# A two-layer RWKV-7 and attention step on one core: GpSimd instead of VectorE makes two products of the recurrence's preparation

## What is computed

```python
def step(S, inp):
    r_t, w_t, k_t, v_t, a_t, b_t = inp
    sa = jnp.einsum('bhvk,bhk->bhv', S, a_t)
    S = S * w_t[:, :, None, :] + sa[..., None] * b_t[:, :, None, :] + v_t[..., None] * k_t[:, :, None, :]
    return S, jnp.einsum('bhvk,bhk->bhv', S, r_t)
```

## Time and profile before

| | |
|---|---|
| time, median of 3 runs | 5512.53 us (5505.92 to 5513.2) |
| time of the profiled execution | 5517.87 us |
| its span | 5516.1 us |
| PE busy in the span | 4655.1 us (84%) |
| DVE busy | 1996.5 us (36%) |
| ACT busy | 1822.5 us (33%) |
| POOL busy | 409.9 us (7%) |
| the two recurrences | about 854 to 1556 us and 3595 to 4300 us |
| instructions L456 and L458 | 32 each, 0.686 and 0.685 us |

### The profile page before, as it was taken

One profiled execution on the slowest core, in us unless ns is written; L12 is line 12 of the kernel. 1 busy time (PEld: TensorE's weight loads), 2 busy tenths in 40 slices (PEclk: granted clock), 3 DMA queues, 4 the chain that ended last, 5 costly groups with the idle time before them and its releaser, 6 DMA issues. The chain is left out here.

```text
span 5516.1 us, 118531 instructions
## 1 busy us (share of the span) xinstructions
PE 4655.1 (84%) x49316; PEld 3793.3 (69%) x49316; DVE 1996.5 (36%) x4592; ACT 1822.5 (33%) x3588; POOL 409.9 (7%) x216
## 2 busy tenths in 40 slices
PE   5999996888968887678969999969889688866789
PEld 4999995887845555453459999958888455553533
DVE  3000004555456665331130000055554566643311
ACT  3000004555544553131130000055555444432211
POOL 1222220000000000000022222100000000000000
PEclk9999997999989997689969999979999899976899
DMA  4111111111011101683431111111110111017834
GB/s 159 69 69 69 69 56 54 37 36 39 20 51 39 38 31 56 211 290 111 135 111 69 69 69 69 50 56 31 41 34 19 49 39 38 31 56 227 275 115 133
DMA packets 240533, 444.16 MB, mean 81 GB/s; under 512 B 36594, under 2 KB 133748, under 8 KB 225908
## 3 DMA queue, kind: packets, MB, share of 16 engines
q1 hardware_dynamic: 216900, 323.26, 18.5%
q10 hardware_dynamic: 23232, 115.16, 5.5%
HBM read 314.54 MB, written 132.32 MB: 81 GB/s over the span
## 5 line engine op out<-in xcount | busy, mean ns | idle before, releaser
L1874 PE MATMUL psum<-h_parts,w_parts 128*128 128x416 f32 x2640 | 930.1, 352 | 24.9 <-POOL w_parts L1793 24.9
L1875 PE MATMUL psum<-h_parts,w_parts 128*128 128x416 f32 x2640 | 926.6, 351 | 0.0
L1876 PE MATMUL psum<-h_parts,w_parts 128*128 128x416 f32 x2640 | 925.8, 351 | 0.0
L1836 DVE COPY arena<-psum 128x416 f32<-128x416 f32 x132 | 78.2, 592 | 1433.8 <-PE psum L1876 1433.8
L1758 ACT ACTIVATE arena<-psum 128x416 f32<-128x416 f32 x198 | 102.7, 519 | 1422.2 <-PE psum L1876 1422.2
L1039 PE MATMUL psum<-arena 128*128 128x512 f32 (+3 forms) x1280 | 546.6, 570 | 19.6 <-DVE arena L986 8.1
L1874 PEld LDWEIGHTS psum<-h_parts,w_parts 128*128 128x128 f32 x2640 | 496.3, 188 | 29.6 <-issue 25.2
L1169 PE MATMUL psum<-arena 128*128 128x512 f32 (+1 forms) x1088 | 475.2, 597 | 38.2 <-DMA arena<-x_cur 38.2
L1876 PEld LDWEIGHTS psum<-h_parts,w_parts 128*128 128x128 f32 x2640 | 496.6, 188 | 6.5
L1875 PEld LDWEIGHTS psum<-h_parts,w_parts 128*128 128x128 f32 x2640 | 497.5, 188 | 4.3
L1169 PEld LDWEIGHTS psum<-arena 128*128 128x128 f32 (+1 forms) x1088 | 201.6, 187 | 310.4 <-issue 310.4
(11 more groups left out here) (336 smaller groups left out, 6618.9 us busy)
## 6 DMA issues: line engine op xcount, KB each, us to landing
out_proj_t<-arena ACTq DMA_DIRECT2D x66, 1040.5 KB, 4.1
arena<-in_cache_k SPq DMA_DIRECT2D x256, 256.0 KB, 3.9
arena<-in_cache_v SPq DMA_DIRECT2D x256, 256.0 KB, 4.1
arena<-in_w_in SPq DMA_DIRECT2D x66, 512.0 KB, 3.5
arena<-x_cur SPq DMA_DIRECT2D x64, 512.0 KB, 5.7
arena<-out_proj_t SPq DMA_DIRECT2D x96, 257.0 KB, 3.2
arena<-out_proj_t SPq DMA_DIRECT2D x24, 1024.0 KB, 8.8
arena<-mixed_t SPq DMA_DIRECT2D x32, 512.0 KB, 5.1
```

The source lines that it names most:

```text
L1874: pe.matmul(bank[g][:, 0:TG], w_hi[u][:, k, :], h_hi[:, k, col], start=(k == 0), stop=False)
L1875: pe.matmul(bank[g][:, 0:TG], w_hi[u][:, k, :], h_lo[:, k, col], start=False, stop=False)
L1876: mm = pe.matmul(bank[g][:, 0:TG], w_lo[u][:, k, :], h_hi[:, k, col], start=False, stop=(k == KT - 1))
```

## The change

VectorE's steps `sV_R` and `sV_K` are gone, and GpSimd runs the same two products in a loop over all 16 units. A new semaphore pair `pG` (steps `sG_R`, `sG_K`) stands for them. GpSimd waits for E and for kf ahead of R, for Ei ahead of K, and from unit 6 on for the output of unit `m - 5`, which read the buffer of RA that is written. Everyone who used VectorE's order to know that R and K were made now waits for `pG`.

```diff
@@ rwkv_scalar, rates @@
                 if m:
                     pV.wait(act, m - 1, sV_B)
+                    pG.wait(act, m - 1, sG_K)
@@ rwkv_gpsimd @@
             pool.memset(E[:, :, :, 0:1], 1.0).then_inc(r_once, 1)
+            for m in range(NU):
+                tq, two = m // 2, slice(m % 2 * 2, m % 2 * 2 + 2)
+                pA.wait(pool, m, sA_E)
+                pV.wait(pool, m, sV_KF)
+                if m >= 6:
+                    yAll.wait(pool, m - 5, 1)
+                pG.inc(pool.tensor_tensor(q4(RA[:, tq % 3, two, 0, :]), q4(xr), E[:, :, :, 1:CH + 1], ALU.mult))
+                pA.wait(pool, m, sA_EI)
+                pG.inc(pool.tensor_tensor(Kf[:, tq % 2, two, :], kf[:, :, :], Ei[:, :, :], ALU.mult))
+                pG.close()
@@ rwkv_vector @@
                 pA.wait(dve, m, {sV_XK: sA_CK, sV_XR: sA_CR, sV_XV: sA_CV}[k])
+                if m and k == sV_XR:
+                    pG.wait(dve, m - 1, sG_R)
...
                     pA.wait(dve, m, sA_MM)
+                    if m:
+                        pG.wait(dve, m - 1, sG_K)
                     i_ = dve.tensor_tensor(kf[:, :, :], tw[:, :, :], xk[:, :, :], ALU.mult)
...
-                elif k == sV_R:
-                    i_ = dve.tensor_tensor(q4(RA[:, tq % 3, two, 0, :]), q4(xr), E[:, :, :, 1:CH + 1], ALU.mult)
-                elif k == sV_K:
-                    i_ = dve.tensor_tensor(Kf[:, tq % 2, two, :], kf[:, :, :], Ei[:, :, :], ALU.mult)
...
                 if m is not None:
-                    prep(m, sV_R)
-                    prep(m, sV_K)
                     prep(m, sV_MX)
                     prep(m, sV_RC)
@@ rwkv_tensor @@
                     pV.wait(pe, n // 2 * 2 + 1, sV_B)
+                    pG.wait(pe, n // 2 * 2 + 1, sG_K)
```

More of the change, by code:

```diff
@@ L223, in build @@
         sA_CK, sA_CR, sA_CV, sA_TW, sA_TA, sA_KS, sA_E, sA_EI, sA_MM, sA_SQ = range(1, 11)
-        sV_XK, sV_XR, sV_XV, sV_LD, sV_SCAN, sV_KF, sV_RKB, sV_R, sV_K, sV_MX, sV_RC, sV_KKN, sV_A, sV_BB, sV_B, sV_BV = range(1, 17)
+        sV_XK, sV_XR, sV_XV, sV_LD, sV_SCAN, sV_KF, sV_RKB, sV_MX, sV_RC, sV_KKN, sV_A, sV_BB, sV_B, sV_BV = range(1, 15)
+        sG_R, sG_K = range(1, 3)
         sT_ZW, sT_ZA, sT_SS, sT_RN, sT_BO = range(1, 6)
-        pA, pV, pT = mark("prep_scalar", 10), mark("prep_vector", 16), mark("prep_tensor", 5)
+        pA, pV, pT, pG = mark("prep_scalar", 10), mark("prep_vector", 14), mark("prep_tensor", 5), mark("prep_gpsimd", 2)
         lA, lV = mark("lora_scalar", 2), mark("lora_vector", 1)
```

## The result

The changed kernel takes 5544.97 us (median of 5 runs, 5539.46 to 5548.31) against 5512.53 us (5505.92 to 5514.15) for the kernel before: a ratio of 1.0059, 95% interval 1.0044 to 1.0074, so 24 to 41 us slower. Its profiled execution has a span of 5543.2 us, 27.1 us more than before.

The account below looks back on a forecast made before the run. It took TensorE as setting the pace, waiting on VectorE's L450, L454, L491, L673 chain. 34.8 us of delay, less 1.8, plus 0.5 at the start gave 33.5 us, so 5546 us, range 5505 to 5561.

Parts of the forecast that it names:

- What bounds the kernel, and that R and K return nothing in the steady part: TensorE sets the pace; in steady slots nobody waits for VectorE's R and K, 1.21 us a unit.
- The second L454 waits for R: In 26 slots VectorE's second L454 stands behind GpSimd's R, 1.34 us late, delaying L491 and TensorE; chance 0.46.
- GpSimd's durations: R and K, each 128 x 512 with two full inputs, take 1.26 us each on GpSimd.
- 26 x 1.34 - 1.8 = 33 us for the steady part: Steady-part loss: 26 slots each 1.34 us late, less 1.84 us that VectorE now waits ahead of L491.
- At the start of the pipeline the two amounts cancel, +0.5 us: In four starting units, 1.21 us saved on VectorE against 1.34 us of delay leaves +0.5 us.
- The waits for GpSimd cost nothing: New waits of TensorE, ScalarE and VectorE for GpSimd are fulfilled long before reached, with over 10 us of slack.
- nothing is shared: Rival: GpSimd and VectorE do not interfere, only the pipeline start counts: -5.3 us, 5507 us; chance 0.24.
- By turns within an instruction: Rival: L454 pair and GpSimd both run slower; at worst its 0.88 us doubles, 21 us, 5533; chance 0.14.
- GpSimd keeps its turn: Rival: R and K run back to back, or R precedes the first L454; L491 2.6 us late, 5578; chance 0.09.
- Faster through the clock: Rival: TensorE's clock rises one unit earlier at the pipeline start, with no contention: 5501 us; chance 0.07.

Follow-up runs that it names:

- rc_release: The changed kernel with GpSimd's R and K released by sV_RC (the reciprocal) instead of sV_KF: 5504.46 us against 5512.59, ratio 0.9983.
- k_late: The changed kernel with only GpSimd's K waiting for sV_RC, R still released by sV_KF: 5527.8 us, ratio 1.0031 to the kernel before.
- products_twice: The kernel before, VectorE still making R and K, with GpSimd making both once more into an unread spare tile: 5555.57 us, ratio 1.0082.
- memset_beside: The kernel before with two GpSimd memsets of 704 columns in a spare tile, where the change has R and K: 5510.84 us, ratio 0.9996.
- memset_long: The kernel before with two GpSimd memsets of 1600 columns in a spare tile, released by sV_KF: 5519.32 us against 5514.31, ratio 1.0013.
- mask_first_after: The changed kernel with VectorE's masked(u, 3) put ahead of sV_RKB: 5515.08 us, ratio 1.0013 to the kernel before.
- rkb_release: The changed kernel with GpSimd's R released by sV_RKB instead of sV_KF: 5501.93 us, ratio 0.9989 to the kernel before.

## Why the prediction was right, and where it was not

The time was right, 5546 predicted and 5545 measured, and so were the sign and the mechanism of the steady part. Two of its terms were wrong by about as much in opposite directions, so that the hit to the microsecond is luck.

- **What bounds the kernel, and that R and K return nothing in the steady part:** right. In rc_release, where nothing meets, the gain is 8 us (3 to 15 by the interval), where the prediction has 5.3 us for that case.
- **The second L454 waits for R:** right, in 31 of 32 units. Its size was not. I had it 1.34 us late, because I added R's whole length to the end of the first L454. In 30 of 32 units R starts 0.13 to 0.16 us after the end of sV_KF and so 0.09 to 0.12 us behind the first of the pair, runs beside it, and the second ends 1.80 us after the pair began: 0.92 us late. TensorE's wait for the mask, forecast near 1.6 us, is 1.23.
- **GpSimd's durations:** R and K take 1.18 and 1.27 us where they meet nothing, 1.42 and 1.45 in the change; predicted was 1.26 for both.
- **26 x 1.34 - 1.8 = 33 us for the steady part:** too large. With 0.92 us it is 22 us, and k_late against rc_release shows 23.7 in their traces. Against the kernel before, the stretch from sV_KF of unit 3 to that of unit 15 grew from 483.1 to 489.8 us in layer 1 and from 484.3 to 495.8 in layer 2, by 18.2 us together.
- **At the start of the pipeline the two amounts cancel, +0.5 us:** this is the step that failed. It missed that K meets the clamp. The sum there moved L461 forward by 1.21 us without asking what GpSimd is at by then; K runs until 3.0 us after the end of sV_KF, and VectorE reaches the clamp at 1.8. The prediction's own times have the same overlap: its second L454 would end at 1.74 + 0.48 = 2.22 us, with K at work until 3.0. It had also read from the earlier trace rows that one input can use both ways into SBUF, but looked only for instructions with two inputs. From sV_KF of unit 0 to that of unit 3, layer 1 went from 940.17 - 874.16 = 66.0 us to 945.72 - 873.41 = 72.3, both layers from 131.9 to 143.4. The clamp's own excess is 2 x (3 x 1.06 + 0.46 + 0.14) = 7.6 us.
- **The waits for GpSimd cost nothing:** right. TensorE never waits for L430 or L432 in the trace after.
- **The rivals:** "nothing is shared" is refuted by products_twice against memset_beside. "By turns within an instruction" is refuted by the rows of the pair (L470): the first keeps 0.49 us with R beside it, the second waits. "GpSimd keeps its turn" did not happen; in the slot shown, the pair's second ends at 1190.13, when K has run for 0.31 of its 1.45 us. "Faster through the clock" did not happen.

What the start of the pipeline lost beyond the clamp's own 7.6 us shows in TensorE's clock. From sV_KF of unit 2 to that of unit 3 the change takes 32.6 us in layer 1 and k_late 28.8, and 1.06 of the 3.8 us are the clamp. The same matmuls in the change and then in k_late, with the granted clock of 914 to 920 us ahead of them:

```profile
914.00:920.00 6.00, 4.90 (x44) 4.17 (x46) 3.85 (x7) 2.56 (x5) 2.74 (x2) 0.50 0.00 0
918.97 1.97 PE L867 MATMUL psum<-arena 64*64 64x64 f32 x32
920.73 1.69 PE L873 MATMUL psum<-ident,arena 64*64 64x64 f32 x32
931.92 1.71 PE L683 MATMUL psum<-arena 64*64 64x64 f32 x32 [1.47 <-DVE arena L503]
...
914.00:920.00 6.00, 5.91 (x116) 4.98 (x112) 3.60 (x7) 3.52 (x9) 0.95 (x1) 0.84 0.01 3
915.49 1.34 PE L868 MATMUL psum<-arena 64*64 64x64 f32 x32
916.67 1.10 PE L874 MATMUL psum<-ident,arena 64*64 64x64 f32 x32
927.26 1.15 PE L684 MATMUL psum<-arena 64*64 64x64 f32 x32 [1.47 <-DVE arena L504]
```

In the change TensorE stays at the lower of its two levels (0.50, 1.2 of 2.4 GHz) through L867 and most of L873, 1.2 us more than in k_late, and is there once more from 932 us on, which by the end of that dip makes another 1.5 us. k_late has such a dip too, only after its unit 3 has begun (L684, 1.53 us at 942.68), so the second amount is moved rather than lost; this fits the 3.2 us that come back in the steady part. The granted clock from 914 to 920 us is 0.50 in all three of the change, memset_long and mask_first_after, in which the clamp is held up, and 0.89, 0.84 and 0.72 in the kernel before, k_late and memset_beside, in which it is not. That the clamp's delay is what keeps the clock down is concluded from this pattern, not tested by itself. The traces thus account for some 10 us of K's meeting; what the medians show beyond that (17) is within their error.

The Trainium skill's rule (SBUF — State Buffer, § Who interferes with whom) is borne out in what it says of instructions with two SBUF inputs, held up by GpSimd's products and not by its memsets. It also says that a `tensor_scalar` can take a mode that uses both of VectorE's ports and then contends with GpSimd; the clamp, held up beside products and memsets alike, fits that, but no row shows in which mode it ran. Where the section says that the one that comes second is fully blocked, the traces agree for VectorE. For GpSimd's R, which starts 0.10 us into a first L470 of 0.48 us and was 0.24 us longer (1.42 against 1.18 us), they can't tell: GpSimd's rows do not show when it first reaches for SBUF.

## What to carry to other kernels

Moving work to an idle GpSimd does not make it free: ask which VectorE instructions will run beside it, and what waits for those. Here those with two SBUF inputs and the clamp, a `tensor_scalar` between SBUF tiles, were held up for the rest of GpSimd's instruction, while the reciprocal between SBUF tiles and those that read PSUM and one SBUF tile went on. The same two products cost 32 us or gained 8 by the placing of one wait, so choose GpSimd's release for the gap that VectorE's own list of instructions shows, and check the first and last units of a pipeline apart from the steady ones.

## What the runs showed of the hardware

- A VectorE instruction with two inputs in SBUF (128 x 256, 0.48 us) that came while GpSimd's R was at work ended 0.28 us after R's row (1190.13 and 1189.85); with a memset of 1.43 us beside it (memset_long), the pair took its usual 0.88.
- A one-input clamp of 8 columns, 0.17 us by itself, took 1.23 us beside a GpSimd product and 0.91 beside a memset, and ended within 0.03 us of GpSimd's end both times. A one-input reciprocal of 8 columns took at most 0.21 us beside either (22 times each, in the change and in memset_long).
- GpSimd pays as well: K took up to 1.78 us in rkb_release, and 1.27 by itself.
- A VectorE instruction that reads PSUM and one SBUF tile took 0.68 to 0.69 us beside either.
